# Small score levels of a gated linear attention as 32 by 32 squares in a compact array, modulation rows moved ahead of each level's scores

## The reference, cut to what matters

```python
def gla_chunked(q, k, v, log_a, s0):          # C = 64, scanned over L // C chunks
    def step(s, inp):
        qc, kc, vc, lac = inp
        g = jnp.cumsum(lac, axis=-2)
        diff = g[..., :, None, :] - g[..., None, :, :]
        decay = jnp.exp(jnp.where(lower, diff, -jnp.inf))
        scores = jnp.einsum('bhik,bhjk,bhijk->bhij', qc, kc, decay)
        o = (jnp.einsum('bhij,bhjv->bhiv', scores, vc)
             + jnp.einsum('bhik,bhkv->bhiv', qc * jnp.exp(g), s))
...
    y_b = from_heads(o).astype(h.dtype) * jax.nn.silu(gate_b)     # o: both directions, rms-normed
...
    m = jax.nn.silu(cond) @ w[:, :n * D_MODEL] + b[:n * D_MODEL]   # modulation of the next block
```

## Time and profile before

| what | value |
|---|---|
| median of three runs | 2442.5 us |
| the profiled execution's own time | 2451.27 us |
| its span (first to last instruction) | 2449.5 us |
| PE busy | 2368.2 us (97%) |
| DVE busy | 1421.7 us (58%) |
| ACT busy | 1112.2 us (45%) |
| chain that ended last | PE 88%, DVE 7%, ACT 3%, DMA 1%, issue 1% |

### The profile page before, as it was taken

How to read it: one execution, slowest core, us unless ns; L and a number is a source line. 1 busy time by engine, 2 the same in 40 slices (tenths; PEclk the granted TensorE clock), 3 DMA queues, 4 the chain that set the end, 5 groups by cost and what they waited for, 6 DMA issues and landing times.

```text
span 2449.5 us, 29750 instructions
## 1 busy us (share of the span) xinstructions
PE 2368.2 (97%) x12180; PEld 1918.3 (78%) x12180; DVE 1421.7 (58%) x1340; ACT 1112.2 (45%) x1170; POOL 66.7 (3%) x108
## 2 busy tenths in 40 slices
PE   5999999999999999999999989999999999999998
PEld 1678878887687888878878877888888888888886
DVE  1245677456846886566667784655555445445454
ACT  1355545344643544546555452455544334334333
POOL 0010010000000000000000100000000000000000
PEclk9899999999999999999999999999999999999999
DMA  9965688567875796555545312654565565565563
GB/s 374 387 217 180 214 287 263 177 182 255 353 250 172 249 371 200 206 189 161 173 153 174 96 27 100 215 172 155 171 189 183 185 197 187 187 195 180 195 209 121
DMA packets 235235, 499.18 MB, mean 204 GB/s; under 512 B 21504, under 2 KB 23616, under 8 KB 228064
## 3 DMA queue, kind: packets, MB, share of 16 engines
q1 hardware_dynamic: 224016, 444.23, 55.0%
q0 software_dynamic: 11088, 53.08, 5.8%
HBM read 492.56 MB, written 4.72 MB: 203 GB/s over the span
## 4 chain that ended last, share of the span: by engine, by line
PE 88%; DVE 7%; ACT 3%; DMA 1%; issue 1%; SPq 0%; DVEq 0%; ACTq 0%
PE banks L2783 76%; PE banks L2856 2%; DMA raw_last_eight<-in_w_ada 1%; PE banks L2879 1%; DVE weights_lo L1625 1%; ACT weights_hi L812 1%; PE banks L3065 1%; PE banks L2935 1%; PE banks L3265 1%; PE banks L2868 0%; PE banks L3028 0%; PE banks L2898 0%; PE banks L3170 0%; DVE inverse_products L2488 0%; DVE decayed_a L1865 0%
## 5 line engine op out<-in xcount | busy, mean ns | idle before, releaser
L1625 DVE TENSOR_TENSOR weights_lo<-weights_raw,weights_hi 128x2048 fp32r<-128x2048 f32 (+1 forms) x356 | 813.4, 2285 | 779.2 <-ACT weights_hi L812 777.5
L812 ACT ACTIVATE weights_hi<-weights_raw 128x2048 fp32r<-128x2048 f32 (+1 forms) x356 | 680.1, 1911 | 987.1 <-PE banks L2783 977.5
L2783 PE MATMUL banks<-weights_hi,acts_hi 128*128 128x512 f32 (+1 forms) x2224 | 879.3, 395 | 10.7 <-DVE weights_lo L1625 10.6
L2783 PE MATMUL banks<-weights_hi,acts_lo 128*128 128x512 f32 (+1 forms) x2224 | 869.1, 391 | 0.0
L2783 PE MATMUL banks<-weights_lo,acts_hi 128*128 128x512 f32 (+1 forms) x2224 | 868.9, 391 | 0.0
L2783 PEld LDWEIGHTS banks<-weights_hi,acts_hi 128*128 128x128 f32 x2224 | 420.8, 189 | 111.0 <-issue 27.3
L2783 PEld LDWEIGHTS banks<-weights_hi,acts_lo 128*128 128x128 f32 x2224 | 420.2, 189 | 87.6
L2783 PEld LDWEIGHTS banks<-weights_lo,acts_hi 128*128 128x128 f32 x2224 | 420.8, 189 | 84.0 <-issue 0.5
L2783 PE MATMUL banks<-weights_hi,hidden_hi 128*128 128x512 f32 x320 | 125.4, 392 | 0.5 <-DVE weights_lo L1625 0.5
L2783 PE MATMUL banks<-weights_hi,hidden_lo 128*128 128x512 f32 x320 | 124.7, 390 | 0.0
L2783 PE MATMUL banks<-weights_lo,hidden_hi 128*128 128x512 f32 x320 | 124.6, 389 | 0.0
(11 more groups left out here) (573 smaller groups left out, 1969.0 us busy)
## 6 DMA issues: line engine op xcount, KB each, us to landing
weights_raw<-in_w_in_e SPq DMA_DIRECT2D x80, 1024.0 KB, 5.4
weights_raw<-in_w_up SPq DMA_DIRECT2D x64, 1024.0 KB, 5.4
weights_raw<-in_w_down SPq DMA_DIRECT2D x64, 1024.0 KB, 5.1
weights_raw<-in_w_in SPq DMA_DIRECT2D x44, 1024.0 KB, 5.1
raw_last_eight<-in_w_ada SPq DMA_DIRECT2D x64, 512.0 KB, 11.6
raw_eight<-in_w_ada SPq DMA_DIRECT2D x32, 1024.0 KB, 7.8
weights_raw<-in_w_in_o SPq DMA_DIRECT2D x32, 1024.0 KB, 5.6
gate_piece<-in_w_ada POOLq DMA_DIRECT2D x32, 512.0 KB, 5.8
```

The lines of the kernel that those rows point to most:

```text
L812: eng.activation(WHI[:, c % 2, :, 0:n], RAW[:, sl, :, 0:n], ACT.Copy).then_inc(hi_ready, 1)
L1625: eng.tensor_tensor(WLO[:, c % 2, :, 0:n], RAW[:, c % 4, :, 0:n], WHI[:, c % 2, :, 0:n].bitcast(F32), ALU.subtract).then_inc(lo_ready, 1)
L2783: ins = eng.matmul(BANKS[:, par * 2 + h, 0:s.n], x[:, t, h * P:(h + 1) * P], w[:, c % 2, k, 0:s.n], start=(kc == 0 and k == 0 and m == 0), ...
```

## The change

Levels 0 to 4 and the diagonal lie within squares of 32 by 32 tokens. PE now forms only these squares, the four of a 128-token half one below the other in a bank's partitions, so that a bank holds 4 x 32 columns in place of 4 x 128. They are collected in a new array `ACCS` (8 x 32), under masks of 32 columns, and ACT copies `ACCS` once into the squares on the diagonal of `ACCD`, between the collection of levels 14 and 15. `ACCD` is zeroed first by POOL, since the parts that no level writes are not written by the diagonal any more. On PE the two modulation rows now stand ahead of the wait for the factors of a level. On DVE the forward state factor moves from n = 11 behind the backward one.

```diff
+    ACCS = place("scores_squares", 77, [P, 2 * HEADS, 32])
...
+    key, query = J_[:, 0:32] % 32, I_[:, 0:32]
+    parts.append(("ident32", (key == query) * 1.0))
...
-            m = (J_ // (2 * b) == I_ // (2 * b)) & (J_ // b % 2 == d) & (I_ // b % 2 == 1 - d)
+            m = (key // (2 * b) == query // (2 * b)) & (key // b % 2 == d) & (query // b % 2 == 1 - d)
... POOL
         eng.memset(ADAR[:, 0:2, :], 0.0).then_inc(S("cond_rows_zeroed"), 1)
-        eng.wait_ge(S("cond_rows_zeroed"), 2)
+        eng.memset(ACCD[:, :, :, :], 0.0).then_inc(S("cond_rows_zeroed"), 1)
+        eng.wait_ge(S("cond_rows_zeroed"), 3)
... ACT, collect_block
+            if (d, l) == (0, 5):
+                eng.wait_ge(S("cond_rows_zeroed"), 3)
... ACT, end of the stage
         collect_block(14)
+        for j in range(2):
+            copied(eng, J["level1_4"] + j)
+        for o in range(0, P, 32):
+            eng.activation(ACCD[o:o + 32, :, :, o:o + 32].rearrange("p a b c -> p (a b) c"), ACCS[o:o + 32, :, :], ACT.Copy)
         collect_block(15)
... DVE, collect
-                            for t in (ACCD[:, 2 * j:2 * j + 2, :, :].rearrange("p a b c -> p (a b c)"), bank(jj))]
-                free(eng.copy_predicated(by_query[0], mask.to_broadcast([P, 4, P // (2 * b), b]).bitcast(I32), by_query[1]), jj)
+                            for t in (ACCS[:, 4 * j:4 * j + 4, :].rearrange("p a b -> p (a b)"), bank(jj)[:, 0:P])]
+                free(eng.copy_predicated(by_query[0], mask.to_broadcast([P, 4, 16 // b, b]).bitcast(I32), by_query[1]), jj)
... DVE, diagonal: 4 x 128 elements a bank become 4 x 32
-                                          in1=ident.rearrange("p (a b) -> p a b", a=1).to_broadcast([P, 4, P]),
+                                          in1=const("ident32").rearrange("p (a b) -> p a b", a=1).to_broadcast([P, 4, 32]),
... DVE, order
                 state_factors(1)
+                state_factors(0)
             if LEVELS[n - 1][1] < 5:
                 collect(n - 1)
-            if n == 11:
-                state_factors(0)
... PE
+        def score_squares(name, A, B, first=0, step=1):
+            for j in range(2):
+                jj = J[name] + j
+                bank_free(eng, jj)
+                for hd in (2 * j, 2 * j + 1):
+                    for h in range(2):
+                        at = 32 * (2 * (hd % 2) + h)
+                        for k2 in range(2):
+                            for o in range(0, P, 32):
+                                i0 = h * P + o
+                                ins = eng.matmul(bank(jj)[o:o + 32, at + first:at + 32:step],
+                                                 A[:, 2 * hd + k2, i0:i0 + 32],
+                                                 B[:, 2 * hd + k2, i0 + first:i0 + 32:step],
+                                                 start=(k2 == 0), stop=(k2 == 1))
+                full(ins, jj)
...
-        scores("diag", KTT, QT)
+        score_squares("diag", KTT, QT)
         for n, (d, l) in enumerate(LEVELS):
             Wn = DECAYED[n]
+            plain_rows(2 * n)
+            plain_rows(2 * n + 1)
             eng.wait_ge(S("factors"), n + 1)
...
+            elif l == 0:
+                score_squares(f"level{d}_{l}", KTT, Wn, 1 - d, 2)
             elif l < 7:
+                score_squares(f"level{d}_{l}", Wn, Wn)
...
-            plain_rows(2 * n)
-            plain_rows(2 * n + 1)
```

More of the change, by code:

```diff
@@ L1920, in _ @@
             bank_full(eng, jj)
-            free(eng.scalar_tensor_tensor(out=ACCD[:, 2 * j:2 * j + 2, :, :].rearrange("p a b c -> p (a b) c"),
-                                          in0=bank(jj).rearrange("p (a b) -> p a b", a=4), scalar=2.0,
-                                          in1=ident.rearrange("p (a b) -> p a b", a=1).to_broadcast([P, 4, P]),
+            free(eng.scalar_tensor_tensor(out=ACCS[:, 4 * j:4 * j + 4, :],
+                                          in0=bank(jj)[:, 0:P].rearrange("p (a b) -> p a b", a=4), scalar=2.0,
+                                          in1=const("ident32").rearrange("p (a b) -> p a b", a=1).to_broadcast([P, 4, 32]),
                                           op0=ALU.mult, op1=ALU.mult), jj)
@@ L3038, in _ @@
                 scores_by_32(f"level{d}_{l}", Wn, d)
+            elif l == 6:
+                scores(f"level{d}_{l}", Wn, Wn, (64 * d, 64 - 64 * d, 64, 1))
+            elif l == 0:
+                score_squares(f"level{d}_{l}", KTT, Wn, 1 - d, 2)
             elif l < 7:
-                scores(f"level{d}_{l}", Wn if l else KTT, Wn,
-                       (64 * d, 64 - 64 * d, 64, 1) if l == 6 else (0, 1 - d, P, 2) if l == 0 else (0, 0, P, 1))
+                score_squares(f"level{d}_{l}", Wn, Wn)
             else:
```

## The result

The changed kernel takes 2455.4 us (median of 7 runs, 2452.6 to 2464.9), the kernel before, timed beside it, 2445.9 us (7 runs, 2441.9 to 2451.3). The ratio is 1.0033, with a 95% interval of 1.0020 to 1.0047: slower by 4.9 to 11.5 us, where the prediction had 2435.6 us, faster, and a range up to 2446. The profiled execution of the changed kernel took 2456.0 us with a span of 2454.2 us.

What follows compares the result with a forecast made beforehand. DVE was taken to pace the levels, PE close behind and setting the end. Gains of 5.7 us (DVE) and 2.8 us (PE's tail), 8.5 us, less 1.6 for the clock gave 6.9 us: 2442.5 to 2435.6 us, range 2432.5 to 2446.

Steps and rivals of the forecast that it cites:

- Scores: PE's score blocks, diagonal and ten levels: 3.77 us falls to 1.0 each, 30 us less, only the tail counting.
- Collections: DVE's masked copies of the scores shrink to a quarter of their elements: 6.0 us saved, between 5.2 and 6.9.
- The end of the stage: Outputs begin at about 665.7 in place of 674.2, set by DVE: 8.5 us, 5.7 from DVE and 2.8 from PE's tail.
- ACT's wait: DVE newly waits at level 7 for ACT's exponentials: about 0.3 us lost, 0 to 0.8.
- ACT's and POOL's additions: ACT's four extra copies, some 1.4 us, and POOL's extra zeroing, 0.96 us, are covered: charged nothing.
- the state factor's move: DVE's 2.53 us leave n = 11 and return behind the last one: zero for DVE's end, cover for PE.
- Chunks: Weight chunks that PE's earlier rows wait for: the last lands near 657, needed before 660.5; price nothing.
- The clock: PE's pause of some 3 us just before the outputs lowers its clock: 1.6 us charged.
- B: Rival, slower: PE at half its clock sets the stage, 2454 us; chance 0.13.
- C: Rival, middle: low clock holds in parts of the stage, gain 1.5 to 4.8 us, 2438 to 2441; chance 0.22.
- E: Rival: the clock does not fall before the outputs, gain 8.5 us, 2434; chance 0.60 together with the forecast.
- the low end: Bottom of the forecast range, 2432.5 us: 6.9 us saved in copies, no fall of the clock, 1 us more.

Runs made afterwards that it cites:

- run 4: The changed kernel with weight chunks 8 to 31 loaded only in 128 of 2048 columns and one of four parts: 2440.4 us in one run.
- run 5: The changed kernel with only the first of two contraction halves of each square formed, so half the matmuls: 2443.8 us in one run.
- 10: The kernel before with each 128 by 128 product issued as four in column groups, and chunks 8 to 31 loaded only in part: 2449.5 us in one run.
- run 6: The changed kernel with squares of 64 in place of 32, nothing left out: 2440.6 against 2448.1 us for the kernel before, ratio 0.9967.
- Run 3: The kernel before with each 128 by 128 product issued as four of 32 rows in four column groups: 2452.7 against 2447.4 us, ratio 1.0026.
- run 1: The kernel before with only the order changed, rows ahead of scores and forward state factor last: 2448.6 against 2447.4 us, ratio 0.9999.

## Why the prediction was wrong, step by step

**The step that failed** is *Scores*: "I take 1.0 ... neither is on the path, because DVE's period stays near 5.3 us and PE then has 1.0 + 1.83 of work in it." The column time of a block was close (1.3 us at the full clock where none is cut in two; 1.0 taken, 1.0 to 2.0 the range). But the number of its instructions was counted only to get that time and never as a load on their supply. It had a path of its own: packets of 16 KB, twice as many, through the DMA engines that the chunks fill. Its price was 28.4 us of pauses, up to 4.4 us each where PE's slack in a level was about 2.4, and with them, and the low clock that followed them, the stage took 95 us in place of 77 (runs 4 and 5, with 10.0 us of pauses and none). That the supply is what pauses PE is shown from both sides, less of other traffic (4, 10) and fewer instructions (5, 6), and by more instructions in whole tiles (3). Where a packet is held before its transfer starts, and why packets keep 3.3 us and more apart even with light loads, where 10.0 us of pauses stay, the runs don't show.

**Collections:** right. DVE's busy time in the stage fell by 5.9 us, 6.0 forecast. The copies L1900 took 224/230/313 ns against 0.23 and 0.30 forecast, the diagonal's 280 to 291 ns against 0.3. **The end of the stage:** right once the pauses are gone. The forecast was 665.7 from a diagonal at 588.4, that is 77.3 us; runs 4 and 5 have 77.3 and 76.9. Run 4 still has 10.0 us of pauses in it, but all except one of 0.73 us lie well ahead of the end, and DVE waits there for PE 0.4 us in all. The two state factors stand back to back, as forecast, with the outputs behind them. **ACT's wait, ACT's and POOL's additions, the state factor's move:** DVE waits 0.6 us for ACT at level 7 in runs 4 and 5 (0.3 taken, 0 to 0.8 the range); nothing else of them is late there.

**Chunks:** in time. After has no wait for them in PE's list, and the measured 404 to 413 GB/s of full stretches in place of 419 were enough. What was missed is that this traffic, which PE's earlier rows make denser (DMA share of the stage 0.97 in run 1, 0.87 before), delays something else.

**The clock:** charged at 1.6 us before the outputs. Runs 1 and 5 show that (run 1 gives 1.7 of its 1.8 us back, run 5 takes 1.6 us longer to `out_e`); the changed kernel itself began its outputs at the full clock, after a pause of only 1.0 us. Ahead of them it was low for 30.7 us. The Trainium skill's rule that pauses between bursts bring the clock down ("TensorE: Matmul & The Clock Gate", "Why this matters for your kernels") points the right way here: the changed kernel's pause of 2.10 us ahead of 595.28 is followed by 10.2 us at 0.50 (fourth window above). Run 6 has an exception.

**The rivals:** B came nearest in time (2454) and in its sign, but by luck, since its mechanism is not what happened. Its condition, 31.5 us of PE's work run at half clock, is 63 us of low clock; 30.7 were measured. B also needs a PE that is full at half clock; PE was busy 63.8 of 95.1 us. Run 3 lost about 6 us with 3.4 us of low clock, and run 5 had 17 us of it with no longer stage. The low clock followed the pauses. How much it adds to the changed kernel's loss was not measured apart from the pauses. Its 0.13 was also too little: each of B, C and E asked what PE's clock does, and none what feeds PE. In the sums, the low end comes out at 2432.1 and not at 2432.5, which changes nothing.

## What to carry to other kernels

Before cutting products into thinner ones, count the instructions as well as the columns: each matmul here comes with a weight load, some 250 records of the two used up a 16 KB packet, and the stage that used them faster while the DMA engines were full got pauses which no semaphore explains. Here 15 packets in 77 us were too many beside the loads, 10 were not. In the profile they read "issue" on PE, and the instruction queue of the DMA view counts the packets. Make the pieces only as small as the engine that sets the pace needs: here the 64 x 64 squares, with half the instructions, took 4.6 us off DVE's busy time (77.3 to 72.7), where squares of 32 took 5.9, and left the loss out.

## What was not expected of the hardware

- Instructions are not supplied for free. The Trainium skill ("Runtime: NRT & Kernel Launch", "Instruction fetch mechanics") says that a refill is in blocks of 16 KiB, which the 15 packets of 0.25 MB agree with, and that fetching is hidden by the rate of issue. That does not hold here: there are 28.4 us of pauses in the changed kernel's stage with the DMA engines 88% busy, and still 10.0 us in run 4 with them 31% busy.
- In four column groups a block of 128 matmuls of 128 x 16 took 1.28 us where it ran through, some 10 ns a matmul, against 2.08 us for 64 in two groups of 64 columns.
- The clock does not fall after each pause of the same length. A pause of 3.16 us ahead of the outputs in run 1 was followed by a window of 3.4 us with a mean of 0.55; one of 3.17 us at the same place in run 6 was not, as the last window shows:

```profile
668.00:671.40 3.40, 3.40 (x16) 3.01 (x17) 2.45 (x2) 3.34 (x5) 0.00 (x0) 1.00 0.00 2
```
